# Mixer A's scores: eight matmuls of whole and half height per query tile in place of twelve half-height ones

## What is computed

```
def diff_attention(q, k, v, lam):          # q, k: (tokens, head, component, 64)
    s = einsum('bqhcd,bshcd->bhcqs', q, k) * 64 ** -0.5
    p = softmax(s, axis=-1)
    p = p[:, :, 0] - lam * p[:, :, 1]
    return einsum('bhqs,bshe->bqhe', p, v)

z = h @ w_in                               # all projections, (640, 2048) @ (2048, 6656)
oa = rms_norm(diff_attention(qa, ka, va, lam), subln_g) * (1 - lam_init)
out = concat([oa * silu(ga), ob * silu(gb)]) @ w_out
```

## Time and profile before

| | |
|---|---|
| median of 3 runs | 1267.07 us (1266.96 to 1267.14) |
| the profiled execution | 1266.19 us, of which the span is 1264.4 us |
| granted TensorE clock, mean | 0.995 |
| TensorE matmuls busy | 1234.2 us, 98% |
| TensorE weight loads busy | 987.7 us, 78% |
| VectorE | 767.9 us, 61% |
| ScalarE | 599.3 us, 47% |
| GpSimd | 258.8 us, 20% |
| the eight scores of mixer A | 32 query tiles of 12 matmuls, 8 of 6 |

### The profile page before, as it was taken

The page is one execution under the profiler, slowest core; times in us unless marked ns, Lnnn a source line. Parts: engine busy times, 40 slices in busy tenths (PEclk is TensorE's granted clock), DMA queues, the critical chain, the costliest instruction groups (busy, mean ns, idle before and its releaser), DMA issues.

```text
span 1264.4 us, 17126 instructions
## 1 busy us (share of the span) xinstructions
PE 1234.2 (98%) x6413; PEld 987.7 (78%) x6413; DVE 767.9 (61%) x1177; ACT 599.3 (47%) x1259; POOL 258.8 (20%) x440
## 2 busy tenths in 40 slices
PE   5899999999999999999999999999999999999996
PEld 4455788888888888788787878888787888888885
DVE  5244578667587776554545364554646665788774
ACT  5232325545555455454555545555555755312223
POOL 2111023012031030212222221222223312211111
PEclk9999999999999999999999999999999999999998
DMA  9999332222221232322222131222224423757644
GB/s 335 383 381 322 96 109 76 60 73 72 76 96 43 70 101 68 91 67 68 75 65 76 51 90 51 81 59 82 60 71 131 137 83 95 250 179 229 190 142 167
DMA packets 130065, 156.45 MB, mean 124 GB/s; under 512 B 8272, under 2 KB 97008, under 8 KB 129216
## 3 DMA queue, kind: packets, MB, share of 16 engines
q1 hardware_dynamic: 116256, 109.12, 26.5%
q0 software_dynamic: 13584, 45.72, 11.6%
q10 hardware_dynamic: 144, 0.52, 0.1%
HBM read 144.18 MB, written 11.16 MB: 123 GB/s over the span
## 4 chain that ended last, share of the span: by engine, by line
PE 95%; DMA 2%; SPq 2%; DVE 0%; ACT 0%; issue 0%; POOL 0%; POOLq 0%; ACTq 0%
PE z_ps L658 26%; PE z_ps L660 24%; PE z_ps L659 24%; PE ring L753 5%; PE ring L788 4%; PE ring L853 4%; PE ring L684 2%; PE ring L857 2%; DMA ada_raw<-in_w_ada_dram 2%; SPq L624 1%; PE ring L659 1%; PE ring L660 1%; PE ring L860 1%; PE ring L658 1%; PE ring L900 0%; PE ring L698 0%
## 5 line engine op out<-in xcount | busy, mean ns | idle before, releaser
L658 PE MATMUL z_ps<-w_hi,xt_hi 128*128 128x512 f32 x1360 | 562.0, 413 | 1.0 <-DVE xt_lo L1463 1.0
L660 PE MATMUL z_ps<-w_hi,xt_lo 128*128 128x512 f32 x1360 | 531.6, 391 | 0.0
L659 PE MATMUL z_ps<-w_lo,xt_hi 128*128 128x512 f32 x1360 | 531.3, 391 | 0.0
L944 ACT ACTIVATE w_hi<-w_raw 128x512 fp32r<-128x512 f32 x272 | 170.7, 628 | 338.8 <-PE z_ps L660 313.2
L1292 DVE TENSOR_TENSOR w_lo<-w_raw,w_hi 128x512 fp32r<-128x512 f32 x272 | 196.8, 727 | 201.3 <-ACT w_hi L944 201.0
L658 PEld LDWEIGHTS z_ps<-w_hi,xt_hi 128*128 128x128 f32 x1360 | 255.8, 188 | 73.1 <-issue 26.1
L660 PEld LDWEIGHTS z_ps<-w_hi,xt_lo 128*128 128x128 f32 x1360 | 255.3, 188 | 55.9
L659 PEld LDWEIGHTS z_ps<-w_lo,xt_hi 128*128 128x128 f32 x1360 | 256.7, 189 | 39.4
L1379 DVE TENSOR_REDUCE small<-s_sb 128x2 f32<-128x1536 f32 (+1 forms) x60 | 88.3, 1472 | 22.4 <-ACT s_sb L944 21.2
L1055 ACT ACTIVATE s_sb<-s_sb,small 128x768 f32<-128x768 f32 (+1 forms) x120 | 97.9, 820 | 2.8 <-DVE small L1379 2.7
L1714 POOL TENSOR_TENSOR sg<-sg,zs 128x128 f32<-128x128 f32 (+1 forms) x60 | 38.3, 638 | 282.2 <-DVE sg L1362 281.6
(11 more groups left out here) (172 smaller groups left out, 1350.2 us busy)
## 6 DMA issues: line engine op xcount, KB each, us to landing
w_raw<-in_w_in_dram SPq DMA_DIRECT2D x186, 256.0 KB, 3.2
ada_raw<-in_w_ada_dram SPq DMA_DIRECT2D x64, 512.0 KB, 12.5
w_raw<-in_w_out_dram SPq DMA_DIRECT2D x64, 256.0 KB, 3.8
gate_raw<-in_w_ada_dram POOLq DMA_DIRECT2D x12, 1024.0 KB, 8.0
w_raw<-in_w_in_dram POOLq DMA_DIRECT2D x22, 256.0 KB, 6.2
out_dram<-y_sb SPq DMA_DIRECT2D x9, 512.0 KB, 3.6
o_spill<-row_st POOLq DMA_DIRECT2D x14, 320.0 KB, 3.0
row_st<-o_spill POOLq DMA_DIRECT2D x14, 320.0 KB, 3.4
```

The costliest lines, as they stand in the source:

```text
L658: pe.matmul(out, hi_l, hi_r, start=start, stop=False)
L659: pe.matmul(out, hi_l, lo_r, start=False, stop=False)
L660: return pe.matmul(out, lo_l, hi_r, start=False, stop=stop)
L944: return act.activation(out, in_, ACT.Copy, **kw)
```

## The change

For mixer A alone, the operands get another layout. There is a tile of 128 partitions for each component: `k_hi[c]` holds the component's high keys in the component's own half of the partitions and its low keys in the other half; `q_hi[c]` holds its high queries in both halves. One full-height matmul of `q_hi[c]` with `k_hi[c]` then gives hi*hi + hi*lo. The third term, lo*hi, stays a half-height matmul of `q_lo[0]`'s half with the half of `k_hi[c]`.

Per query tile 1 to 4 there are now 4 full-height matmuls (`whole`) and 4 half-height ones (`low`), for tile 0 two and two. `tail_done` is now raised by component 0's `low` on the tail, and component 1's `low` on the tail waits for it.

For the layout, each of the four copies of `qk_his` becomes two of 64 partitions, and each of the four subtractions of `qk_los` two of 64 partitions. Two copies of 64 partitions and 640 columns are added on VectorE, which write the second copy of the high queries; they raise a new semaphore `q_twice`, for which the scores of tile 0 wait. QK moves from step 3 to step 2.

```diff
+STEPS_D = {s: work for s, work in STEPS.items() if s != 3}
+STEPS_D[2] = [("QK", 0)]
...
-                for c_, of_tail, i in ((0, 0, 0), (1, 1, 0), (1, 1, 1), (0, 0, 1), (1, 1, 2), (1, 0, 0), (0, 0, 2), (1, 0, 1),
-                                       (0, 1, 0), (0, 1, 1), (1, 0, 2), (0, 1, 2)):
-                    if of_tail:
-                        if c_ == 0 and i == 0:
-                            pe.wait_ge(tail_done, tails)
...
+                def whole(out, c_, k0, kn, start=True):
+                    pe.matmul(out, q_hi[c_][:, q0:q0 + P], k_hi[c_][:, k0:k0 + kn], start=start, stop=False,
+                              skip_group_check=True)
+
+                def low(out, c_, k0, kn, turn=None):
+                    rows = HALVES[c_]
+                    ins = pe.matmul(out, q_lo[0][rows, q0:q0 + P], k_hi[c_][rows, k0:k0 + kn], start=False, stop=True,
+                                    skip_group_check=True)
...
+                for c_ in range(2):
+                    whole(tail[c_], c_, 512, NKEY - 512, start=(c_ == 0))
+                for c_ in range(2):
+                    whole(main[c_], c_, 0, 512)
+                low(tail[0], 0, 512, NKEY - 512).then_inc(tail_done, 1)
+                low(main[1], 1, 0, 512, n + 1)
+                low(main[0], 0, 0, 512, n)
+                pe.wait_ge(tail_done, tails)
+                low(tail[1], 1, 512, NKEY - 512, n + 2)
...
+                    if t == 0:
+                        pe.wait_ge(q_twice, 2 * (a - D_IT + 1))
...
             def qk_his(a):
+                if group_kind(a) == "D":
+                    for of, n, col, w, at_col in qk_halves(a):
+                        wait_full(act, n)
+                        for c_, rows in enumerate(HALVES):
+                            dst = (q_hi if of == "q" else k_hi)[c_]
+                            copy(dst[rows, at_col:at_col + w], RB(n)[rows, col:col + w]).then_inc(qk_hi_done, 1)
+                    return
...
             def qk_los(a):
+                        for c_, rows in enumerate(HALVES):
+                            hi = (q_hi if of == "q" else k_hi)[c_]
+                            out = q_lo[0][rows, cols] if of == "q" else hi[HALVES[1 - c_], cols]
+                            ins = dve.tensor_tensor(out, RB(n)[rows, col:col + w], hi[rows, cols].bitcast(F32), ALU.subtract)
...
+                    for c_, rows in enumerate(HALVES):
+                        dve.tensor_copy(q_hi[c_][HALVES[1 - c_], :], q_hi[c_][rows, :].bitcast(F32)).then_inc(q_twice, 1)
```

More of the change, by code:

```diff
@@ L96 @@
 }
-LAST_STEPS = dict(STEPS)
+STEPS_D = {s: work for s, work in STEPS.items() if s != 3}
+STEPS_D[2] = [("QK", 0)]
+LAST_STEPS = dict(STEPS_D)
 LAST_STEPS[10] = [("T", 2), ("S", 4)]
@@ L123, in steps_at @@
         return [("QK", KV_IT, 0)] if s == KV_QK_STEP else []
-    for kind, t in (LAST_STEPS if it == OUT_IT else STEPS).get(s, []):
+    for kind, t in (LAST_STEPS if it == OUT_IT else STEPS_D if group_kind(it - 1) == "D" else STEPS).get(s, []):
         a = it - 1
@@ L412, in build @@
         qk_hi_done = sem("qk_hi_done")
+        q_twice = sem("q_twice")
         v_hi_done, v_lo_done = sem("v_hi_done"), sem("v_lo_done")
@@ L493, in qk_parts, with qk_halves @@
                 [(n + 2, P * c, P, q_hi[c][:, S:S + P], q_lo[c][:, S:S + P], c == 1) for c in range(2)]
-        QKP = [len(qk_parts(a)) for a in range(OUT_IT)]
+        LOW, HIGH = slice(0, DK_A), slice(DK_A, P)
+        HALVES = (LOW, HIGH)
+        def qk_halves(a):
+            n = TURN[("QK", a, 0)]
+            S, C = LAT * P, PAST * P
+            return [("q", n, 0, S, 0), ("k", n + 1, 0, S, 0), ("k", n + 2, 0, C + P, S), ("q", n + 2, C + P, P, S)]
+        QKP = [8 if group_kind(a) == "D" else len(qk_parts(a)) for a in range(OUT_IT)]
         def t_parts(a, t):
@@ L782, in s_pair @@
                 q0 = P * (t - 1) if t else LAT * P
[L783 to L790, removed]
+                def whole(out, c_, k0, kn, start=True):
[5 more added lines that the diff above has]
+                                    skip_group_check=True)
+                    if turn is not None:
                         filled(ins, turn)
@@ L795, in s_pair @@
                     outs = [claim(n + c_)[:, 0:P] for c_ in range(2)]
-                    for i in range(3):
-                        for c_ in range(2):
-                            product(outs[c_], c_, i, NKEY, P, n + c_)
+                    for c_ in range(2):
+                        whole(outs[c_], c_, NKEY, P)
+                    for c_ in range(2):
+                        low(outs[c_], c_, NKEY, P, n + c_)
                     return
@@ L1365, in qk_los @@
                 q0 = sum(QKP[:a])
+                if group_kind(a) == "D":
+                    halves = qk_halves(a)
+                    for i, (of, n, col, w, at_col) in enumerate(halves):
+                        dve.wait_ge(qk_hi_done, q0 + (2 * i + 2 if n != halves[-1][1] else QKP[a]))
+                        cols = slice(at_col, at_col + w)
+                        for c_, rows in enumerate(HALVES):
+                            hi = (q_hi if of == "q" else k_hi)[c_]
+                            out = q_lo[0][rows, cols] if of == "q" else hi[HALVES[1 - c_], cols]
+                            ins = dve.tensor_tensor(out, RB(n)[rows, col:col + w], hi[rows, cols].bitcast(F32), ALU.subtract)
+                        if i != 2:
+                            ins.then_inc(free_sem(n), 1)
+                    for c_, rows in enumerate(HALVES):
+                        dve.tensor_copy(q_hi[c_][HALVES[1 - c_], :], q_hi[c_][rows, :].bitcast(F32)).then_inc(q_twice, 1)
+                    return
                 turns = [part[0] for part in qk_parts(a)]
```

## The result

The changed kernel takes 1272.54 us (median of 5 runs, 1271.03 to 1274.86) against 1267.14 for the kernel before (5 runs, 1266.96 to 1267.51): a ratio of 1.0044, 95% interval 1.0033 to 1.0055. It is slower by 5.4 us. The prediction had 1269.9, so +2.8, in a range from 1263.0 to 1273.5, and slower as the likeliest side: right in sign and range, too small by half. The profiled execution took 1273.24 us, its span is 1271.4 at a mean granted clock of 0.996.

The account below looks back on a forecast made before the run. TensorE, busy for 98% of the span, was taken to bound the kernel. Tiles 1 to 4 at +3.2 us and tile 0 at -0.4 gave +2.8 on 1267.07, so 1269.9, in a range from 1263.0 to 1273.5.

Parts of the forecast that it names:

- The columns are the same, one way in, one way out, so merging brings nothing by itself: Score tiles 1 to 4 of mixer A: 1.04 us of columns as before, so merged products alone gain nothing.
- The new tile, +0.10: Mixer A's tiles 1 to 4: 2.10 us against 2.00, the `tail_done` wait now uncovered at the end; +3.2 us over 32.
- Which value between the bounds: Wait for `tail_done`: middle value +3.2 us taken, between -3.5 without any wait and +6.7 with the marker held up.
- The rival by which it waits for the long matmul beside it: `tail_done` held up by the 512-column matmul running beside its own: +6.7 us in the tiles, 1273.4 in all; chance 0.10.
- the free wait: Rival: waiting for `tail_done` costs nothing, so merging makes the kernel faster by 3.5 + 0.4, to 1263.2; chance 0.12.
- the hidden load: Rival: the last tail's weight load hides behind running columns, -3.2 us against the forecast, 1266.7, no change; chance 0.10.
- Tile 0, -0.4 us: First score tile of each mixer A head: 1.08 us against 1.14, -0.06 in each of 8, -0.4 us together.
- QK earlier, cost 0: QK's transposes in step 2, 3.4 us earlier, with 1.9 us to spare after the rotation: no cost on TensorE.
- More copies, cost 0 with 1.5 us to spare: Added ScalarE and VectorE work ends at 596.9, tile 0's scores start at 598.47: 1.5 us left, no cost.
- `q_twice` comes late: Rival: TensorE stands at tile 0 of each head, up to 1.2 us a head, 1280 in all; chance 0.05.
- The sum: Whole kernel: +3.2 us for tiles 1 to 4 and -0.4 for tile 0 make +2.8, a median of 1269.9.
- The range: Whole kernel's time: 1263.0, without a wait, to 1273.5, with the marker held; the forecast's own range is +1.5 to +4.3.

Follow-up runs that it names:

- 1: Changed kernel with the low-part matmuls full-height too, over zeros cleared in the first head, and no `tail_done`: 1262.99 us, 0.9977 of the kernel before.
- 3: Changed kernel with component 1's main moved ahead of component 0's marked tail: 1276.47 us, 1.0080 of the kernel before.
- 6: Kernel before with only QK of mixer A's heads moved to step 2: 1267.9 us, ratio 1.0000.
- 9: Kernel before with QK in step 2, copies and subtractions in halves and two unread copies more, old score tiles: 1267.29 us, ratio 0.9999.
- 7: Changed kernel with QK back in step 3: 1318.08 us, 1.0401 of the kernel before.

## Why the prediction was right, and where it was short

- *The columns are the same, one way in, one way out, so merging brings nothing by itself*: right. The changed tile is 1.04 of columns again, and 1 shows what would have brought something: no transition at all.
- *The new tile, +0.10*: right, each mark within 0.01 in the tile shown; in the mean +0.12, so +3.7 us in place of +3.2.
- *Which value between the bounds*: right, and shown by 3. The marker keeps program order. The rival by which it waits for the long matmul beside it is refuted (0.45 us, read rightly), and so are the free wait and the hidden load.
- *Tile 0, -0.4 us*: right (1.09 against 1.14, 8 times).
- *QK earlier, cost 0*: right, to the 1 us that 6 can show.
- *More copies, cost 0 with 1.5 us to spare*: the cost is right (no wait of TensorE for these copies; 9), the margin was 0.45. Two steps failed. One is that only the last part's chain counts. VectorE works without a break from the first low part to the last copy:

```profile
593.41 1.39 DVE L1398 TENSOR_TENSOR q_lo<-ring,q_hi 64x512 fp32r<-64x512 f32 x2 [0.95 <-ACT q_hi L961]
594.83 2.55 DVE L1398 TENSOR_TENSOR k_hi<-ring,k_hi 64x512 fp32r<-64x512 f32 x4
597.40 0.59 DVE L1398 TENSOR_TENSOR q_lo<-ring,q_hi 64x128 fp32r<-64x128 f32 x2
```

  So the whole queue of ten operations sets the end, not the last transposes; that took 0.8 us of the margin. The other is the time at which TensorE asks: the old half-height load started 0.32 behind the last projection matmul, the new full-height one starts with it (599.48). The rival "`q_twice` comes late" had the right place. Its price left out the clock, which in 7 added 2.8 us to a delay of 3.1; at the 1.2 us that it allowed for, experiment 1 shows no fall of the clock.
- *The sum*: +2.8 forecast. The terms named measure +3.7 - 0.4 = +3.3. What was missing: 0.03 us a tile behind the tile (1.0 us in all) and 1.5 us in the rest. With them it is 5.8; the medians have 5.4, the spans 6.0. For the rest the prediction said that the change of TensorE's own time, "plus any new wait", is the whole effect, and then looked for new waits only around the score tiles. Neither missing term has a cause that is shown.
- *The range*: +5.4 lies outside the forecast's own range of +1.5 to +4.3. It lies in the stated range only because that reaches to the rival of the held marker, 1273.4, which is nearer to the measured 1272.5 than the forecast is and which 3 refutes. So the sign came for the reason given; that the time fell into the range was in part luck.

## What to carry to other kernels

When matmuls of half height stand among full-height ones, count the transitions before the columns: here a way in and out costs 0.4 us, as much as 900 columns, and doing everything at full height over zeros is 0.27 us a tile faster than the mix. Put a marker that another piece waits for as early as possible, and keep independent columns behind it; behind a wait at the end nothing is covered. And price a margin that is missed by the clock too: a delay of 3.1 us cost 5.9, one of 1.2 us only itself. Last, compare more than one profile of each kernel, and cut the span into stretches: a quarter of this slowdown lies 80 us and more behind the code that was changed.

## What was not expected of the hardware

- Operations on 64 partitions take as long as on 128: VectorE's 64x640 copy 0.49 us against 0.50 for 128x640. Two halves cost twice.
- One execution can have the projection matmuls behind every tile 0.02 us longer in sum than another of the same program (539.9 and 540.9 us for the same tiles).
- One block of 512 columns landed after 5.0 us in one kernel and after 7.7 in the other, at a place where their programs are alike. The long issue (1.13 us in place of 0.43) can't be the whole reason: four of the six profiles with the old tiles have an issue of 1.4 to 2.0 us in the same stretch, and their rest is not longer for it.
